# Two norms from one residual: both sums of squares taken together, and the scaled residual written later

## What is computed

```python
# first block
x = x + gt2 * conv_ffn(h, w_up, conv_w, conv_b, w_down)
x = x * rsqrt(mean(x * x) + 1e-6) * norm_f_w
# second block
h = x * rsqrt(mean(x * x) + 1e-6) * g_mix * (1 + sc1) + sh1
proj = h @ w_in
...
x = x + gt1 * mix
```

## Time and profile before

| | us |
|---|---|
| median of three runs | 2411.75 |
| lowest and highest | 2410.09, 2411.97 |
| profiled execution, first to last instruction | 2412.6 |
| PE busy in it | 2214.5 |
| DVE busy | 1143.3 |
| ACT busy | 737.0 |
| POOL busy | 217.7 |

### The profile page before, as it was taken

One profiled execution on the slowest core, in us unless ns is written; L12 is line 12 of the kernel. 1 busy time (PEld: TensorE's weight loads), 2 busy tenths in 40 slices (PEclk: granted clock), 3 DMA queues, 4 the chain that ended last, 5 costly groups with the idle time before them and its releaser, 6 DMA issues.

```text
span 2412.6 us, 41218 instructions
## 1 busy us (share of the span) xinstructions
PE 2214.5 (92%) x17720; PEld 1576.1 (65%) x17720; DVE 1143.3 (47%) x2011; ACT 737.0 (31%) x1107; POOL 217.7 (9%) x97
## 2 busy tenths in 40 slices
PE   7999898989989999988989999979899999699994
PEld 5485858585436889765668888857645677456563
DVE  4545454543657565344567774243355643511113
ACT  2323222221441222254343332252234532422222
POOL 0020202020000000000123434410000000000001
PEclk9999999999989999999999999989999999899997
DMA  8201010102446566200423332245120133479994
GB/s 254 88 4 48 8 40 17 39 18 85 146 140 227 163 204 187 64 1 18 140 70 92 100 87 96 96 76 143 31 83 18 44 101 105 181 290 405 404 417 167
DMA packets 216315, 295.27 MB, mean 122 GB/s; under 512 B 7640, under 2 KB 191872, under 8 KB 207968
## 3 DMA queue, kind: packets, MB, share of 16 engines
q1 hardware_dynamic: 210784, 274.85, 33.8%
q0 software_dynamic: 3072, 9.74, 1.9%
q10 hardware_dynamic: 2304, 8.39, 0.9%
HBM read 279.84 MB, written 13.11 MB: 121 GB/s over the span
## 4 chain that ended last, share of the span: by engine, by line
PE 79%; DVE 8%; ACT 5%; DMA 4%; issue 2%; SPq 1%; POOL 0%; POOLq 0%; ACTq 0%; DVEq 0%
PE ps L661 11%; PE ps L1148 10%; PE ps L766 10%; PE ps L989 8%; PE ps L957 6%; PE ps L1179 5%; PE ps L1359 4%; PE ps L1206 3%; PE ps L1013 3%; DMA ring<-in_w_up 3%; PE ps L1043 2%; PE ps L1059 2%; PE ps L1332 2%; PE ps L1130 2%; PE ps L1380 2%
## 5 line engine op out<-in xcount | busy, mean ns | idle before, releaser
L766 PE MATMUL ps<-arena 64*64 64x64 f32 x7168 | 227.7, 222 | 15.4 <-POOL arena L1912 8.8
L766 PEld LDWEIGHTS ps<-arena 64*64 64x64 f32 x7168 | 222.5, 138 | 20.2 <-POOL arena L1912 9.6
L661 PE MATMUL ps<-hT,ring 128*128 128x512 f32 (+1 forms) x480 | 212.7, 599 | 3.1 <-ACT hT L1430 2.4
L1918 POOL TENSOR_TENSOR w_low<-ring,w_high 128x2048 fp32r<-128x2048 f32 x22 | 102.0, 4634 | 828.3 <-ACT w_high L1672 828.3
L661 PEld LDWEIGHTS ps<-hT,ring 128*128 128x128 f32 (+1 forms) x480 | 89.9, 189 | 120.3 <-issue 117.6
L1148 PE MATMUL ps<-h_high,w_low 128*128 128x512 f32 x352 | 140.1, 398 | 7.1 <-DVE h_low L2333 7.0
L1148 PE MATMUL ps<-h_low,w_high 128*128 128x512 f32 x352 | 140.6, 399 | 0.0
L1148 PE MATMUL ps<-h_high,w_high 128*128 128x512 f32 x352 | 140.0, 398 | 0.0
L1456 ACT ACTIVATE arena<-ps 128x512 f32<-128x512 f32 x104 | 62.1, 597 | 211.5 <-PE ps L766 201.3
L2239 DVE CUSTOM_DVE_ANT_0 arena<-ps,arena 128x256 f32<-128x256 f32 (+3 forms) x160 | 67.0, 468 | 124.8 <-PE ps L1059 124.7
L2056 DVE TENSOR_TENSOR arena<-ps,arena 128x512 f32<-128x512 f32 x88 | 60.9, 692 | 119.4 <-PE ps L766 119.2
(11 more groups left out here) (410 smaller groups left out, 4397.3 us busy)
## 6 DMA issues: line engine op xcount, KB each, us to landing
ring<-in_w_in SPq DMA_DIRECT2D x54, 1024.0 KB, 5.3
arena<-in_w_ada SPq DMA_DIRECT2D x80, 512.0 KB, 4.0
arena<-in_w_down SPq DMA_DIRECT2D x32, 1024.0 KB, 9.2
ring<-in_w_gate SPq DMA_DIRECT2D x30, 1024.0 KB, 9.5
ring<-in_w_up SPq DMA_DIRECT2D x30, 1024.0 KB, 11.0
ring<-in_w_up SPq DMA_DIRECT2D x44, 512.0 KB, 5.0
ring<-in_w_down SPq DMA_DIRECT2D x8, 1024.0 KB, 5.0
y_scratch<-arena ACTq DMA_DIRECT2D x16, 512.0 KB, 7.8
```

Of the source, the lines that this page charges most:

```text
L661: mm = pe.matmul(dst, w[:, k, hf * P:hf * P + width], rhs(k), start=(start and k == 0), stop=(stop and k == kts - 1))
L766: mm = pe.matmul(ps[r, bank, cc], l[r, cc], x[r, 0:64] if x is eye64 else x[r, cc], start=(i == 0), stop=(i == len(terms) - 1))
L1918: pool.tensor_tensor(W_LOW[:, slot_, :], ring[:, slot_, :], W_HIGH[:, j % 2, :].bitcast(F32), ALU.subtract).then_inc(w_low, 1)
```

## The change

- ACT makes `WEIGHED` = sqrt(norm_f_w^2 + 1e-6) once, at the start of the kernel, from a square that DVE makes.
- While down runs, each residual tile is squared twice on ACT: with scale `WEIGHED` into a ring of three buffers of `SQUARES`, and plainly into `hT`. DVE adds up both kinds (`add_both`).
- PE multiplies both sums by ones, the weighed one first (bank 7), the plain one second (bank 6). ACT takes the root of the weighed sum with 1e-12 as its addend: this is the root for the apply loop, whose gain now also holds `norm_f_w`.
- in2 tiles 0 and 1 are rounded by ACT after the last weight tile of down and before the squares of tiles 6 and 7; DVE makes their low parts after residual tile 5. They have buffers of their own.
- The root of the plain sum is taken after the apply loop (`RSTD_F`). The scaling of `xT` in place is cut in eight (`carry`) and put between DVE's emptyings of in2.
- The eight squares of the second norm, its eight products with ones, and the eight scalings ahead of it are gone from their place.

```diff
-        IN2_W_HIGH = [... for i, at in enumerate((14848, 28672))]
+        IN2_W_HIGH = [... for i, at in enumerate((18944, 20992, 14848, 28672))]
 # PE
-            norm_total(2)
-            norm_sum(3)
+            pe.wait_ge(squares_added, ADDED_AT[2] + 2 * (KT - 1) - 1)
+            pe.matmul(ps[:, 7, :], ones, SQUARES[:, 0, :], start=True, stop=True).then_inc(summed, 1)
+            norm_total(2, ADDED_AT[2] + 2 * (KT - 1))
 # ACT
             act.wait_ge(consts_made, 1)
+            lg(act.activation(WEIGHED, WEIGHED, ACT.Sqrt, bias=EPSC))
             act.wait_ge(got_x, 16)
...
+            def square_both(k):
+                act.wait_ge(freed["D"], BEFORE["down"]["D"] + k + 1)
+                if k >= 4:
+                    act.wait_ge(squares_added, ADDED_AT[2] + 2 * (k - 3) - 1)
+                act.activation(SQUARES[:, 1 + (k - 1) % 3 if k else 0, :], xT[:, k, :], ACT.Square,
+                               scale=WEIGHED[:, k:k + 1]).then_inc(squared, 1)
+                act.activation(hT[:, k, :], xT[:, k, :], ACT.Square).then_inc(squared, 1)
...
             for d in range(2, 12):
                 down_weights_high(d)
                 for k in range(2 * (d // 3) - 2, 2 * (d // 3)) if d % 3 == 1 else ():
-                    norm_square(k, freed["D"], BEFORE["down"]["D"] + k + 1)
+                    square_both(k)
+            in2_weight_high(0)
+            in2_weight_high(1)
             for k in (6, 7):
-                norm_square(k, freed["D"], BEFORE["down"]["D"] + k + 1)
-            norm_root(2)
-            for k in range(KT):
-                norm_square(k, norm_applied, APPLIED_AT[2] + k + 1)
-            in2_weight_high(0)
-            in2_weight_high(1)
-            norm_root(3)
+                square_both(k)
+            act.wait_ge(summed, 3)
+            lg.done(act.activation(RSTD, ps[:, 7, :], ACT.Ln, scale=1.0 / D, bias=EPS_SQUARED))
+            act.activation(RSTD, RSTD, ACT.Exp, scale=-0.5, bias=ZERO).then_inc(rooted, 1)
             (apply loop)
+            act.wait_ge(summed, 4)
+            lg.done(act.activation(RSTD_F, ps[:, 6, :], ACT.Ln, scale=1.0 / D, bias=EPSC))
+            act.activation(RSTD_F, RSTD_F, ACT.Exp, scale=-0.5, bias=ZERO).then_inc(rooted, 1)
             act.wait_ge(angled, 1)
 # DVE
+            lk.done(tt(WEIGHED, col("norm_f_w", 0, 8), col("norm_f_w", 0, 8), ALU.mult))
...
+            def add_both(k):
+                for i, (total, square) in enumerate(((SQUARES[:, 0, :], SQUARES[:, 1 + (k - 1) % 3, :]), (hT[:, 0, :], hT[:, k, :]))):
+                    dve.wait_ge(squared, SQUARED_AT[2] + 2 * k + i + 1)
+                    if k >= 2:
+                        dve.wait_ge(squares_added, ADDED_AT[2] + 2 * (k - 2) + i + 1)
+                    tt(total, total, square, ALU.add).then_inc(squares_added, 1)
...
                     if i >= 2:
-                        add_square(k_norm, i - 1)
-                add_square(k_norm, 7)
+                        add_both(i - 1) if phase == "down" else add_square(k_norm, i - 1)
+                    if phase == "down" and i == 5:
+                        in2_weight_low(0)
+                        in2_weight_low(1)
+                add_both(7) if phase == "down" else add_square(k_norm, 7)
...
-            dve.wait_ge(rooted, 3)
-            for k in range(KT):
-                stt(xT[:, k, :], xT[:, k, :], col("norm_f_w", k), RSTD, ALU.mult, ALU.mult).then_inc(norm_applied, 1)
             gain(mod2, 0, col("g_mix_2", 0, 8))
-            in2_weight_low(0)
-            in2_weight_low(1)
-            dve.wait_ge(rooted, 4)
+            lk.done(tt(GAIN, GAIN, col("norm_f_w", 0, 8), ALU.mult))
+            def carry(k):
+                stt(xT[:, k, :], xT[:, k, :], col("norm_f_w", k), RSTD_F, ALU.mult, ALU.mult).then_inc(norm_applied, 1)
+            dve.wait_ge(summed, 4)
+            dve.wait_ge(rooted, 3)
             (apply loop)
             in2_weight_low(2)
+            dve.wait_ge(rooted, 4)
             for o in range(1, 13, 2):
                 psum_out("in2", IN2[o], ps[:, o % 4, :], in2_value(o))
                 in2_weight_low(o // 2 + 3)
+                carry(o // 2)
             for o in (13, 15):
                 c, hf = divmod(o - 13, 2)
                 psum_out("in2", VB[...], tok2(ps[:, o % 4, :]), in2_value(o))
+                carry(o // 2)
...
+            dve.wait_ge(norm_applied, APPLIED_AT[2] + KT)
             residual("w_out2", mod2[:, 16:24], 4, last_weight=15)
```

More of the change, by code:

```diff
@@ L280, in build @@
         H4_HIGH, H4_LOW = [rounded("h4_" + n, offset_of["arena"] + at * 4, KT, T) for n, at in (("high", 6656), ("low", 10752))]
-        IN2_W_HIGH = [rounded(f"in2_w_high_{i}", offset_of["arena"] + at * 4, SLOT)[:, :] for i, at in enumerate((14848, 28672))]
+        IN2_W_HIGH = [rounded(f"in2_w_high_{i}", offset_of["arena"] + at * 4, SLOT)[:, :] for i, at in enumerate((18944, 20992, 14848, 28672))]
         def in2_weight(i):
@@ L286, in in2_weight @@
             size = SLOT // 2 if i == 2 else SLOT
-            return m, IN2_W_HIGH[i % 2][:, 0:size], ring[:, m % R, 0:size], W_LOW[:, m % R, 0:size]
+            return m, IN2_W_HIGH[i if i < 2 else 2 + i % 2][:, 0:size], ring[:, m % R, 0:size], W_LOW[:, m % R, 0:size]
         H2T = area(4096, 4, D)
@@ L319, in build @@
         EPSC, GNC, ZERO, ONE, ZSINK = [small[:, i:i + 1] for i in range(5)]
+        EPS_SQUARED = small[:, 16:17]
+        WEIGHED = small[:, 80:88]
+        SQUARES = area(16896, 4, T)
+        RSTD_F = area(34304, T)
         NM, DEN = [small[:, at:at + 4].rearrange("p (a b) -> p a b", b=2) for at in (6, 10)]
@@ L324, in build @@
         PLS = [small[:, 64:72], small[:, 72:80]]
-        ZERO8 = small[:, 80:88]
         RSTD = sb("rstd", [P, T])[:, :]
@@ L357, in build @@
         squares_added = sem("squares_added")
-        ADDED_AT = {1: 0, 2: KT - 1, 4: 2 * (KT - 1)}
+        ADDED_AT = {1: 0, 2: KT - 1, 4: 3 * (KT - 1)}
+        SQUARED_AT = {0: 0, 1: KT, 2: 2 * KT, 4: 4 * KT, 5: 5 * KT}
         norm_scaled, norm_applied = sem("norm_scaled"), sem("norm_applied")
-        SCALED_AT, APPLIED_AT = {1: 0, 3: 8, 4: 16}, {1: 0, 2: 8, 3: 16, 4: 24}
+        SCALED_AT, APPLIED_AT = {1: 0, 3: 8, 4: 16}, {1: 0, 3: 8, 2: 16, 4: 24}
         h_high, w_high, w_low = [sem(n) for n in ("h_high_made", "weights_high_made", "weights_low_made")]
@@ L676, in norm_sum @@
                 for k in range(first, last):
-                    pe.wait_ge(squared, KT * k_norm + k + 1)
+                    pe.wait_ge(squared, SQUARED_AT[k_norm] + k + 1)
                     mm = pe.matmul(ps[:, 6, :], ones, hT[:, k, :], start=(k == 0), stop=(k == KT - 1))
@@ L680, in norm_sum, with norm_total @@
                     mm.then_inc(summed, 1)
-            def norm_total(k_norm):
-                pe.wait_ge(squares_added, ADDED_AT[k_norm] + KT - 1)
+            def norm_total(k_norm, added=None):
+                pe.wait_ge(squares_added, added or ADDED_AT[k_norm] + KT - 1)
                 pe.matmul(ps[:, 6, :], ones, hT[:, 0, :], start=True, stop=True).then_inc(summed, 1)
@@ L1735, in _ @@
                 up_silu(jj, *ident_)
-            for d in range(2, 12):
-                down_weights_high(d)
-                for k in range(2 * (d // 3) - 2, 2 * (d // 3)) if d % 3 == 1 else ():
-                    norm_square(k, freed["D"], BEFORE["down"]["D"] + k + 1)
-            for k in (6, 7):
-                norm_square(k, freed["D"], BEFORE["down"]["D"] + k + 1)
-            norm_root(2)
-            if stop < 5:
-                return
-            for k in range(KT):
-                norm_square(k, norm_applied, APPLIED_AT[2] + k + 1)
+            def square_both(k):
[5 more added lines that the diff above has]
+                act.activation(hT[:, k, :], xT[:, k, :], ACT.Square).then_inc(squared, 1)
             def in2_weight_high(i):
@@ L1758, in in2_weight_high @@
                 act.activation(high, full_, ACT.Copy).then_inc(in2_w_high, 1)
+            for d in range(2, 12):
+                down_weights_high(d)
+                for k in range(2 * (d // 3) - 2, 2 * (d // 3)) if d % 3 == 1 else ():
+                    square_both(k)
             in2_weight_high(0)
             in2_weight_high(1)
-            norm_root(3)
+            for k in (6, 7):
+                square_both(k)
+            act.wait_ge(summed, 3)
+            lg.done(act.activation(RSTD, ps[:, 7, :], ACT.Ln, scale=1.0 / D, bias=EPS_SQUARED))
+            act.activation(RSTD, RSTD, ACT.Exp, scale=-0.5, bias=ZERO).then_inc(rooted, 1)
+            if stop < 5:
+                return
             h_value = [0] * KT
@@ L1974, in _ @@
             lk(dve.memset(GNC, GN_EPS))
+            lk(dve.memset(EPS_SQUARED, EPS * EPS))
             dve.memset(ZERO, 0.0).then_inc(dve_link, 1)
@@ L2302, in add_square @@
             def add_square(k_norm, k):
-                dve.wait_ge(squared, KT * k_norm + k + 1)
+                dve.wait_ge(squared, SQUARED_AT[k_norm] + k + 1)
                 if k >= 2:
```

(8 more changed lines are left out.)

## The result

| kernel | median us | lowest to highest | runs |
|---|---|---|---|
| before | 2411.86 | 2401.16 to 2415.89 | 20 |
| changed | 2416.31 | 2404.23 to 2422.97 | 20 |

The ratio is 1.0022, interval 1.0013 to 1.0031: slower by 0.1 to 0.3%, at the border of what I had called no change. The forecast was 2410.4 with a range up to 2414.0; the median lies 2.3 us above the range. The profiled execution has a span of 2413.1 us and an own time of 2414.93, so 1.8 us lie around the span.

What follows compares the result with a forecast made beforehand. PE was taken as the bound (79% of the chain), with in2 tile 4's load tied to the table's write. 2412.6 - 1.3 (start) - 13.2 (norms) + 13.2 (tile 4) = 2411.3, less 0.85 gives 2410.4; range 2396.5 to 2414.

Steps and rivals of the forecast that it cites:

- The load waits for the table, not for its issue: In2 tile 4's load lands when the position table's write ends, however early issued; PE resumes at 1662.9.
- gets nothing from them for 23 us: Half of in2 tile 4's load gets nothing for 23 us from the DMA engines that the table's write holds.
- The chain between down and in2, 13.2 us: From the last residual addition to the apply loop, the second norm leaves the path: loop starts 13.2 us earlier.
- The 0.5 for the weighed addition: Before the first norm's chain, one more DVE addition ahead of tile 7's weighed one costs 0 to 0.74, taken as 0.5.
- Work moved into down, carries, plain root: 0: Extra squares, casts and additions in down, eight carries in in2 and the later plain root cost 0, covered by idle time.
- in2: a single stop of about 16 us: Ahead of in2 tile 4, PE's stop grows from 3.08 to 16.3 us, giving the 13.2 back whole.
- The start, 1.3: At the kernel's start, Sqrt loads its table while ACT waits for x, so the squares start 1.28 us sooner.
- Rival 1, engines taking turns: In in2, held engines take turns, tile 4 lands by its issue, 13.2 kept: 2397 us; chance 0.27 with its half form.
- Rival 2, half the clock for the whole tile: After the stop at in2 tile 4, PE stays at half clock, 8.5 us more: 2419 us; chance 0.05.
- PE bounds what follows, so it is kept: The 1.28 us gained at the kernel's start carries through, since PE bounds everything after it.
- The clock: After the longer stop at in2 tile 4, the half-clock stretch may cost 0.8 us less, or more; taken as 0.
- The median of the runs is 0.85 below the span: Last step of the sum: 0.85 us off the execution's 2411.3 gives the forecast median of 2410.4.

Runs made afterwards that it cites:

- a_early: Changed kernel with the position table's write moved to the first attention, so no write runs beside in2: 2399.45 us, ratio 0.9954.
- b_early: Kernel before with the position table's write moved to the first attention, so no write runs beside in2: 2413.64 us, ratio 1.0024.
- a_spread: Changed kernel with the table's 20 KB row sent to DRAM first, then spread by one DMA with the 128 rows outermost: 2395.17 us, ratio 0.9937.
- b_spread: Kernel before with the table's 20 KB row sent to DRAM first, then spread by one DMA, 128 rows outermost: 2406.40 us, ratio 0.9984.
- a_nostart: Changed kernel with its Sqrt moved from the kernel's start to ahead of down's loop: 2414.83 us, ratio 1.0032.
- b_again: Kernel before, unaltered, measured against itself; three such comparisons together gave +0.9 us with a standard error of 0.95.
- b_third: Kernel before, unaltered, measured against itself again; three such comparisons together gave +0.9 us with a standard error of 0.95.

## Why the prediction was wrong, step by step

- *The load waits for the table, not for its issue*: right. Issued at 1616.98, 14.9 us earlier than before, tile 4 is cast at 1655.31, only 3.3 earlier; and without the long write there is no stop (a_early, b_early, a_spread, b_spread). But "gets nothing from them for 23 us" was read from 3 us of rows, and is wrong for the end: from 1648.6 the ring's queue moved one packet for each of the table's.
- *The chain between down and in2, 13.2 us*: right to 0.1 (19.84 - 6.66 = 13.18). The 0.5 for the weighed addition is in it: from the last residual addition to the first instruction on the normalized tile it is 6.66 us, before 1599.24 - 1593.12 = 6.12.
- *Work moved into down, carries, plain root: 0*: right. ACT still idles 8.85 us before the square of tile 6, and the stretch of b_early less that of a_early is 13.2, with all of that work in it.
- *in2: a single stop of about 16 us*: 14.69 us of idle on PE, since the table is done 1.3 earlier than before and the cast follows it by 1.4 us instead of 3.4. The stretch is 126.5 against 126.2, so the 13.2 are given back whole. In part that is luck: the stop came out 1.6 us shorter than the sum had it, and the stop's lower clock costs about 1.5 more than in the usual execution of before.
- *The start, 1.3*: 1.67 on DVE in the one pair of profiles, about 1.3 in the mean of nine against eight for the first product of the first block.
- *Rival 1, engines taking turns*: its outcome is refuted, its mechanism is not. Tile 4, posted early in the write, got 520 packets by 1622, none until 1628.18, and was cast behind the table. But from 1633.7 the ring's queue did get turns, 176 packets for the table's 176, and they were too small to bring the tile in. The Trainium skill ("DMA: Bandwidth & Descriptors", section "Queues, rings and completion order") has an engine change queue after a packet of typically 9 to 17 descriptors, with 64 as the ceiling. The trace agrees that queues are served in turn; its turn of one 5 KB packet is far below the typical figure, though under the ceiling, and the pause of 6 us before stays unexplained.
- *Rival 2, half the clock for the whole tile*: refuted: 3.55 us at the lower clock, where the whole tile would have been 22.6.

The forecast of -1.3 us against the kernel before came out as +4.5 (2416.31 against 2411.86). About 1 of the difference of 5.8 is in any comparison here, 0.3 is the stretch; the rest is in none of the sum's terms. The step that failed is the zero that the working gave to everything outside them: "PE bounds what follows, so it is kept" for what is won at the start, and "*The clock.* ... I take 0". Two points of the last sum need a word.

The first is "The median of the runs is 0.85 below the span". I took that from one profiled execution and three runs as a property of the kernel. It isn't: 1.8 us lie around the span in the executions here, executions of the kernel before spread over 2398 to 2424 us, and the profiled one was 2.9 longer than the others (129.1 against 126.2) in the very stretch that I summed over. Put on the median, the sum is 2411.75 - 1.3 = 2410.45, the same number by luck. So this did not make the miss, but taking one execution's span for the kernel made the range too narrow above: it ended 3.6 us over the forecast, while the median of before alone moved between 2408.1 and 2411.9 from one comparison to the next.

The second is the clock, put at 0 for the one stop and not considered anywhere else. The loss of some 3 us over a change of nothing is likely real (four comparisons, 3.2 with a standard error of 1.15), isn't the start's Sqrt (a_nostart), and goes with a granted clock lower by 0.004. That is large enough, as an estimate: 0.004 x 2411 = 9.6 us of full clock not granted, and some 0.0015 of the 0.004 is only the stop itself, during which the clock reads low and PE has nothing to do (17 us of clock missing in 1590 to 1740 against 9 to 14 before); the other 0.0025 could cost up to 6 us. In the time between executions of one kernel the two go together as well (correlation -0.75 to -0.93 in the kernels with 12 or more executions), which does not say which of them makes the other.

It is tempting to blame the long stop, since the loss does not show in a_spread's comparison with before. The record does not bear that out. With the 1.3 of the start, the changed kernel falls short of its profile's account by about 4 us (-1.3 + 0.3 expected, +3.2 found). a_spread falls short of b_spread by as much (-13.5 - 1.3 expected, -10.6 found) with no stop in either; a_early and b_early, also without one, show none (-13.2 - 1.3 expected, -14.0 with a standard error of 2.4 found). No run lengthened a stop by itself, and none took the extra squares and additions out of down while it kept the rest, so those stand as an untested rival. What makes the 3 us stays open.

## What to carry to other kernels

When a stop further on is set by a transfer, find out what that transfer waits for before you count a gain ahead of it: if it hangs on something else's end, everything won in front is given back. Then look at that something first: here a short second transfer in the table's write made the 13.2 us of the change real in this stretch and added some 2.5 (15.7 - 13.2), a ratio of 0.9937 instead of 1.0022. When two queues share an engine, count how long the other's packets are, not only whether turns are given. And before a forecast of less than 0.2% take the spread of the kernel against itself, not one execution; a comparison of a kernel with itself read up to 1.0013 here.

## What the runs showed of the hardware

- A DMA that reads from 8 partitions kept 8 of 16 engines for 55 us for 2.56 MB, and the half of a load that lay on those engines landed only with its end: no ring packet at all from 1622 to 1628.18, then one for each packet of the write (176 and 176 in 18.6 us). The same bytes from DRAM, ordered so that the 128 rows are outermost, took 13.3 us, and loads beside them landed in 5.4.
- SP's issue blocks when loads wait. In the changed kernel the third waiting one held SP for 18.55 us, until the table's end, where it had been 5.30:

```profile
1633.78 18.55 SPq L490 DMA_DIRECT2D ring<-in_w_in  x1
```

- In two executions of the kernel before, nearly equal stops ahead of in2 tile 4 (3.08 us and 3.04 us in b_again) were followed by 5.7 us at half the clock in the one and by the full clock (1.00) in the other.
- After equal stops of 3.22 us the next 192 products took 45.0 us in one execution and 47.7 in others. In the first 5.5 us behind the stop the granted clock is 1.00 in b_third and 0.50 in the changed kernel's profile; the kernel before itself has both lengths. So the granted clock is not decided by the program alone, and one profile does not tell a kernel's share of it.
- Square on ACT needed no table load of its own behind Sqrt: the eight squares start at 30.40, the moment x is there.
